# Filling TensorE's waits with idle products in the setup, and a weight split moved behind the third feature tile

## The reference

```
r = lax.rsqrt(jnp.mean(xf * xf, axis=-1, keepdims=True) + EPS)
h = (xf * r).astype(x.dtype) * g            # rmsnorm(x, norm_mix[0])
bg, cg, xv = jnp.split(h @ sc_w_in, 3, axis=-1)   # 1024 x 3072
```

## Time and profile before

| | |
|---|---|
| median of 3 runs | 1394.62 us (1393.7 to 1395.48) |
| profiled execution | 1394.49 us |
| its span | 1392.9 us |
| TensorE busy | 1348.9 us, 97% |
| VectorE, ScalarE busy | 727.9 us (52%), 528.3 us (38%) |
| mean granted clock | 0.989 |

### The profile page before, as it was taken

How to read it: one execution, slowest core, us unless ns; L and a number is a source line. 1 busy time by engine, 2 the same in 40 slices (tenths; PEclk the granted TensorE clock), 3 DMA queues, 4 the chain that set the end, 5 groups by cost and what they waited for, 6 DMA issues and landing times.

```text
span 1392.9 us, 27664 instructions
## 1 busy us (share of the span) xinstructions
PE 1348.9 (97%) x11153; PEld 1312.0 (94%) x11153; DVE 727.9 (52%) x1170; ACT 528.3 (38%) x839; POOL 21.2 (2%) x50
## 2 busy tenths in 40 slices
PE   6999999999999999999999899997999999999998
PEld 5999999999999999999889798886899999999998
DVE  4655466555555533344654545547665555553222
ACT  4322244333333322233554444545443333332121
POOL 0000000000000000000000000000000000000000
PEclk9999999999999999999999999999899999999999
DMA  6344435663454354544646426338134443445331
GB/s 174 92 152 152 151 110 161 209 175 106 130 167 152 104 166 135 161 133 150 176 125 199 140 84 190 120 119 261 31 106 149 152 150 105 151 149 161 100 94 62
DMA packets 256585, 195.16 MB, mean 140 GB/s; under 512 B 6581, under 2 KB 250789, under 8 KB 255362
## 3 DMA queue, kind: packets, MB, share of 16 engines
q1 hardware_dynamic: 253528, 139.17, 35.2%
q0 software_dynamic: 1792, 54.43, 10.8%
q10 hardware_dynamic: 1194, 0.54, 0.1%
HBM read 186.60 MB, written 65.21 MB: 181 GB/s over the span
## 4 chain that ended last, share of the span: by engine, by line
PE 91%; DVE 2%; SPq 2%; DMA 2%; issue 1%; ACT 1%; DVEq 0%
PE acc L1529 79%; PE acc L1557 2%; DMA skv<-new_rows 1%; PE N L1518 1%; PE N L1749 1%; SPq L516 1%; PE M L1701 1%; PE acc L1813 1%; PE M L1518 1%; PE acc L1518 1%; PE acc L1709 1%; DMA wraw<-in_sc_w_in_dram 1%; PE M L1813 1%; DVE wl L1030 1%; SPq L512 0%
## 5 line engine op out<-in xcount | busy, mean ns | idle before, releaser
L1529 PE MATMUL acc<-hh,wh 128*128 128x260 f32 x2288 | 468.6, 286 | 10.8 <-DVEq L1304 10.3
L1529 PE MATMUL acc<-hh,wl 128*128 128x260 f32 x2288 | 462.7, 284 | 0.0
L1529 PE MATMUL acc<-hl,wh 128*128 128x260 f32 x2288 | 461.8, 283 | 0.0
L715 ACT ACTIVATE wh<-wraw 128x1024 fp32r<-128x1024 f32 (+1 forms) x212 | 220.5, 1040 | 594.9 <-PE acc L1529 583.1
L1529 PEld LDWEIGHTS acc<-hh,wh 128*128 128x128 f32 x2288 | 355.0, 189 | 14.5 <-DVEq L1304 11.9
L1529 PEld LDWEIGHTS acc<-hh,wl 128*128 128x128 f32 x2288 | 354.2, 189 | 0.0
L1529 PEld LDWEIGHTS acc<-hl,wh 128*128 128x128 f32 x2288 | 353.6, 189 | 0.0
L1030 DVE TENSOR_TENSOR wl<-wraw,wh 128x1024 fp32r<-128x1024 f32 (+1 forms) x212 | 254.2, 1199 | 173.7 <-ACT wh L715 170.9
L1529 PE MATMUL acc<-yh,wh 128*128 128x260 f32 x848 | 173.1, 285 | 5.2 <-DVE x L1440 5.2
L1529 PE MATMUL acc<-yh,wl 128*128 128x260 f32 x848 | 171.2, 283 | 0.0
L1529 PE MATMUL acc<-yl,wh 128*128 128x260 f32 x848 | 171.0, 283 | 0.0
(11 more groups left out here) (218 smaller groups left out, 1108.6 us busy)
## 6 DMA issues: line engine op xcount, KB each, us to landing
out_dram<-in_cache_kv_d_dram POOLq DMA_DIRECT2D x24, 1364.0 KB, 6.3
wraw<-in_ffn_w_gate_dram SPq DMA_DIRECT2D x44, 512.0 KB, 3.9
wraw<-in_ffn_w_up_dram SPq DMA_DIRECT2D x44, 512.0 KB, 3.9
wraw<-in_attn_w_qkv_dram SPq DMA_DIRECT2D x36, 512.0 KB, 4.2
out_dram<-in_cache_kv_d_dram POOLq DMA_DIRECT2D x8, 2044.0 KB, 8.6
wraw<-in_ffn_w_down_dram SPq DMA_DIRECT2D x32, 448.0 KB, 3.8
wraw<-in_sc_w_in_dram SPq DMA_DIRECT2D x24, 512.0 KB, 3.9
wraw<-in_ffn_w_down_dram SPq DMA_DIRECT2D x16, 512.0 KB, 4.0
```

The source lines that it names most:

```text
L715: nc.scalar.activation(wh[c % 2][:, 0:k], wraw[:, c % 4, 0:k], ACT.Copy).then_inc(hi_done, 1)
L1529: ins = T.matmul(acc[:, par, h2, 0:HALF], w[c % 2][:, k, :], a[:, k0 + k, h2, :], start=(first and k == 0 and n == 0), stop=(last and k == ...
```

## The change

TensorE gets `warm(n)`: n plain f32 products of the identity matrix with itself, 128x128, into a part of chunk 1's accumulator that is not in use yet; nothing reads them. Two stand behind the transposes of tile 0 and of tile 1, eight behind those of tile 2, three behind those of tiles 3 and 4. The split of chunk 1 moves: on ScalarE from behind the high half of tile 1 to behind the square of tile 2, on VectorE from the head of m = 1 to the head of m = 3. Accordingly TensorE starts chunk 1 at m = 3 instead of 2, so that three of its steps, not two, stand behind the loop.

```diff
@@ ScalarE
-                if m < 2:
-                    split_hi(S_IN, 0, m)
+                if m == 0:
+                    split_hi(S_IN, 0, 0)
                 act.wait_ge(ssq_ready, m + 1)
                 nc.scalar.activation(sq if m else ssq[:], x[:, m], ACT.Square).then_inc(sq_ready, 1)
+                if m == 2:
+                    split_hi(S_IN, 0, 1)
@@ VectorE
-                if m < 2:
-                    split_lo(S_IN, 0, m)
+                if m == 0:
+                    split_lo(S_IN, 0, 0)
+                if m == 3:
+                    split_lo(S_IN, 0, 1)
@@ TensorE
+            def warm(n):
+                for _ in range(n):
+                    T.matmul(acc[:, 1, 1, 0:P], ident[:], ident[:], start=True, stop=True)
+
             for m in range(2):
                 x_transpose(m)
+                warm(2)
             free_acc(S_IN, 0, 0)
             free_acc(S_IN, 0, 1)
             for m in range(DK):
                 if m + 2 < DK:
                     x_transpose(m + 2)
+                if m == 0:
+                    warm(8)
+                elif m < 3:
+                    warm(3)
                 pe.wait_ge(hl_ready, m + 1)
                 if m == 0:
                     pe.wait_ge(split_done, 5)
                 ins = k_step(acc[:, 0], 0, m, hh, hl, m == 0, m == DK - 1)
                 if m == DK - 1:
                     ins.then_inc(chunk_used, 1)
-                if m == 2:
+                if m == 3:
                     pe.wait_ge(split_done, 6)
-                if m >= 2:
-                    k_step(acc[:, 1], 1, m - 2, hh, hl, m == 2, False)
+                if m >= 3:
+                    k_step(acc[:, 1], 1, m - 3, hh, hl, m == 3, False)
+            k_step(acc[:, 1], 1, DK - 3, hh, hl, False, False)
             k_step(acc[:, 1], 1, DK - 2, hh, hl, False, False)
             k_step(acc[:, 1], 1, DK - 1, hh, hl, False, True).then_inc(chunk_used, 1)
```

## The result

The changed kernel takes 1386.09 us in the median of 4 runs (1385.64 to 1388.18), the kernel before 1395.05 in 4 (1393.7 to 1395.93): a ratio of 0.994, 95% interval 0.9922 to 0.9957, 9.0 us less by the medians and 8.4 by the ratio. I had forecast 3 us less and a range whose lower end was 1390.2. The profiled execution took 1385.64 us. Two executions far off the rest, one of 2647 us (the change with 46 tiny products) and one of 2156 us (the kernel before beside it), are in no median and no ratio here.

What follows compares the result with a forecast made beforehand. TensorE, 97% busy, was taken to bound the kernel, slow and waiting in its first 35 us. Profiled 1394.49 us minus a 3.1 us setup gain gave 1391.4, plus 0.13 for the median 1391.5; range 1390.2 to 1396.0.

Steps and rivals of the forecast that it cites:

- Prices: Cost of one idle product in the setup: taken as 0.22 us warm and 0.44 cold.
- the lower bound: Idle product's price if only its columns' streaming counts: 0.22 us warm, 0.44 cold.
- The dearer price: Rival: weight loads not hidden, idle product 0.88 us cold, 0.44 warm; time about 1395; chance 0.08.
- Clock: Idle products in the setup raise TensorE's clock: earliest at 9.8 us, latest 15.9, taken as 12.0.
- The walk: Setup schedule step by step up to the mean-square products: end 32.2 us instead of 35.0 with the rise at 12.0.
- The waits of 1.2, 1.15 and 1.5 us: New waits the change was forecast to leave in the setup, with no clock loss of their own priced in.
- my 3.1: Middle of the forecast setup gain, 2.3 to 3.8 us, for a clock rise from 9.8 to 13.0.
- Falling back: Rival: the clock falls back in the setup's new waits (1.2, 1.15, 1.5 us); given no chance of its own.
- The step that failed: Opening claim: the change is worth only how much the setup's end at 35.01 us moves; the rest moves forward with it.

Runs made afterwards that it cites:

- 46 tiny: Changed kernel plus 46 products of two weight and two data columns ahead of the mean-square products; second run ratio 0.9994, median 1394.01 us.
- 64 tiny: Kernel before plus 64 two-column products (256 instructions) in TensorE's idle time ahead of the first step; ratio 1.0005.
- before again: Kernel before, unchanged, profiled a second time; ratio 0.9998, median 1395.22 us.
- split only: Kernel before with chunk 1's split moved as in the change, no idle products; ratio 0.999, median 1392.96 us.
- 18 tiny: Kernel before plus 18 two-column products (72 instructions) in TensorE's idle time ahead of the first step; ratio 0.9974, median 1392.02 us.
- split and 18 tiny: Kernel before with the split moved and 18 two-column products, no full-size idle products; ratio 0.9960.
- products only: Kernel before with the change's idle products, chunk 1's split left at m = 1; ratio 0.9973, median 1391.17 us.
- 144 more: Changed kernel plus 18 more full-size idle products ahead of the mean-square products; ratio 0.9979, median 1392.32 us.
- the version without the threes: Changed kernel without the two runs of three idle products; ratio 0.9959, median 1389.8 us.
- the one with earlier products: Changed kernel with its 18 idle products redistributed, five ahead of early transposes, nine behind tile 2, no threes; ratio 0.9963, median 1389.71 us.
- the second trace of the change: Changed kernel, unchanged, run once more with more rounds; ratio 0.9939, median 1387.44 us.

## Why the prediction was wrong

- **Prices.** Idle product 0.22 warm, 0.43 cold: right, the lower bound. The dearer price, 0.44 warm, is refuted. The Trainium skill (TensorE: Matmul & The Clock Gate, Terms) has the transpose mode four times faster for FP32, by which the dearer price would have come; the trace does not agree, since an idle product takes 0.22 us warm and a transpose 0.11.
- **Clock.** The idle f32 products do raise it. Rise at 9.5 in one trace (I had 9.8 as the earliest) and 12.3 in another (12.0).
- **The walk.** Dense end forecast 31.2 for a rise at 9.8 and 32.2 for 12.0; measured 31.00 and 32.47. The waits of 1.2, 1.15 and 1.5 us were 0.78, 0.99 and 1.45. The moved split cost nothing, as said. With the measured 4.0 in place of my 3.1 the sum would have given 1390.6, still inside my range: the setup is not what took the result out of it.
- **Falling back.** I gave it no chance of its own. It does not happen in the setup of the full change, but it does in both halves of it, behind waits of 1.00 and 2.21 us, and in a later stage in three of fourteen traces.
- **The step that failed** is in the first paragraph: "the rest of the program moves forward with it", "what the change is worth is by how much that moment moves". It moves, but another 4.4 to 6 us are gained behind the setup, a term that my sum put at nothing because the program behind the setup is the same. With the code's pages as before, the parts behind the dense end take, by the ratios less the shift of the dense end, +0.1 (64 tiny), -0.2 (before again), -0.7 (split only) and +0.3 us (46 tiny; -1.3 without its cold stretch) against the kernel before. With 72 instructions more they take -4.4 (18 tiny), -3.4 (split and 18 tiny), -2.3 (products only) and, in the change itself, -4.4 and -6.0; with 144 more -3.6. The intervals of the ratios alone are 1.3 to 2.4 us to either side, and the dense end is that of one trace, which moved by 1.5 us between the two traces of the change. Two do not fit so well: the version without the threes (48 more) has -1.6, the one with earlier products (72 more) -1.1, which is no more than their tails give. So about half of the 8.4 to 9.0 us came from neither the clock nor the split, and most of that half goes with the place of the code.
- **What is shown and what is open.** Shown: the 72 instructions alone bring 3.6 us, a full page brings nothing. 0.9 to 1.3 us of it are the tail, and here the traces leave no doubt: in the six with the packet among the output's issues the tail is 5.79 to 6.20 us and one issue of SyncE, the one during which the packet starts, takes 1.56 to 1.79 us; in the eight others the tail is 4.85 to 4.87 and no issue takes over 0.66. Open: the other 2 to 3 us. The first and largest step between the first two traces is in a wait of the attention stage for rows that go out to DRAM and come back. VectorE waits for them and TensorE for VectorE, in the kernel before

```profile
681.55 1.23 DVE L1350 TENSOR_TENSOR skv<-skv 128x1024 f32<-128x1024 f32 x1 [5.15 <-DMA skv<-new_rows]
...
683.56 0.51 PE L1529 MATMUL acc<-hh,wh 128*128 128x260 f32 x2 [1.60 <-DVEq L1304]
```

and in the first trace of the change, where TensorE goes on at 677.62 without idle time,

```profile
675.17 1.23 DVE L1354 TENSOR_TENSOR skv<-skv 128x1024 f32<-128x1024 f32 x1 [2.77 <-DMA skv<-new_rows]
```

In the second trace of the change TensorE is idle there for 1.22 us:

```profile
682.16 0.51 PE L1533 MATMUL acc<-hh,wh 128*128 128x260 f32 x2 [1.22 <-DVEq L1308]
```

The attention stage scatters by 3 us between executions of one kernel. From the dense end to TensorE's last product the traces with the pages moved take 1348.2 to 1352.6 us and the others 1351.0 to 1355.4 (the longest has 1.3 us of cold stretch behind its 46 tiny products in it); the averages are some 2 us apart, but the two groups overlap. The traces also tell where the packets fall. In all six traces with the pages as before no packet of code starts in the 12 us ahead of this wait's end (the next comes 1.0 to 1.7 us behind it), and yet TensorE's product at the wait's end starts 1.25 to 2.32 us after the one before it. In the eight others a packet starts 1.3 to 5.4 us ahead of the end, and that distance is 0.03 to 1.76 us. So a packet in the middle of the transfers, the mechanism of the tail, is not what makes this wait long in the kernel before. What does was not found.

## What to carry to other kernels

Plain f32 products on data at hand raised TensorE's clock before the dense work came. They pay where the wait that they fill is there anyway. A wait behind them can lose the clock again: it was lost behind 1.00 and 2.21 us here and kept through 1.45, so take more than one trace before counting on it. When an edit changes the number of instructions, compare the traces behind the edit as well. Control with as many tiny instructions in idle time, and with one full page of them, and see that the tiny ones do not themselves cost the clock, as the 46 did. A few microseconds of such a gain may be the code's place, and the next edit can take them away.

## What was not expected of the hardware

- A 16 KB packet of code in the middle of the output's transfers went with one SyncE issue of 1.56 to 1.79 us instead of at most 0.66, and with a tail 0.9 to 1.3 us longer, in all six traces that had it and in none of the eight others.
- The clock fell to half behind waits of 1.00 and 2.21 us in two traces (at 20.69 and about 17.3 us), and stayed up through waits of 0.99 and 1.45 us in the change. In these traces the length of the wait in front does not settle alone whether it falls.
- 46 products of two columns, 2.4 us long and between dense products, were followed by 3.4 us at half pace, in both traces of that kernel.
- The granted-clock column reads 1.00 before its first recorded change, while products run at the pace of 1.2 GHz (0.43 us a pair).
